# First expert's rows by products of 0/1 lists, experts of tiles 0 to 2 chosen ahead, weights not held back

## The reference

```python
def hier_moe(t, w_group, b_group, w_expert, b_expert, w_gate, w_up, w_down):
    g_logits = t @ w_group + b_group              # 4 groups
    g_w, g_idx = lax.top_k(softmax(g_logits), 1)
    e_logits = (t @ w_expert + b_expert).reshape(T, 4, 4)
    e_sel = take_along_axis(e_logits, g_idx)      # 4 experts of the group
    e_w, e_idx = lax.top_k(softmax(e_sel), 2)     # two of them
    weights = g_w * e_w / sum(e_w)
    for e in range(16):
        hdn = silu(t @ w_gate[e]) * (t @ w_up[e])     # 1024 -> 512
        y = y + combine[:, e:e+1] * (hdn @ w_down[e]) # 512 -> 1024
    return y
```

## Time and profile before

| | |
|---|---|
| median of 3 runs | 1140.63 us (1140.46 to 1142.6) |
| profiled execution | 1143.3 us, span 1141.5 us |
| PE busy | 1078.8 us (95% of the span), mean granted clock 0.98 |
| DVE, ACT, POOL busy | 508.6, 282.6, 265.0 us |
| DMA | 283.24 MB, mean 248 GB/s |
| expert stages | about 264 to 516 us (layer 0) and 850 to 1101 us (layer 1) |

### The profile page before, as it was taken

One profiled execution on the slowest core, in us unless ns is written; L12 is line 12 of the kernel. 1 busy time (PEld: TensorE's weight loads), 2 busy tenths in 40 slices (PEclk: granted clock), 3 DMA queues, 4 the chain that ended last, 5 costly groups with the idle time before them and its releaser, 6 DMA issues.

```text
span 1141.5 us, 17926 instructions
## 1 busy us (share of the span) xinstructions
PE 1078.8 (95%) x7469; PEld 647.0 (57%) x7469; DVE 508.6 (45%) x939; ACT 282.6 (25%) x461; POOL 265.0 (23%) x373
## 2 busy tenths in 40 slices
PE   6999999999999999996999999999989999999991
PEld 5688887874444433342788877777844444344430
DVE  3465237545533233326422357763355432343317
ACT  4442344320000000004232227763210000000012
POOL 1200012004333443123000013340023344433131
PEclk9899999999999999998999999999989999999996
DMA  9443311248999999998223210004279999999965
GB/s 322 127 146 112 106 38 74 110 186 331 402 422 421 422 423 423 423 418 288 102 75 111 79 69 1 2 1 166 71 263 415 419 421 421 422 423 423 423 230 198
DMA packets 68699, 283.24 MB, mean 248 GB/s; under 512 B 15048, under 2 KB 15216, under 8 KB 44064
## 3 DMA queue, kind: packets, MB, share of 16 engines
q1 hardware_dynamic: 47440, 239.32, 52.3%
q0 software_dynamic: 15232, 38.69, 9.4%
q10 hardware_dynamic: 5968, 4.40, 1.2%
HBM read 259.96 MB, written 22.41 MB: 247 GB/s over the span
## 4 chain that ended last, share of the span: by engine, by line
PE 81%; DVE 6%; DMA 4%; issue 4%; POOL 4%; ACT 1%; SPq 0%; POOLq 0%; DVEq 0%
PE ps L1843 41%; PE ps L1510 11%; PE ps L1512 10%; PE ps L1511 10%; DMA w_f<-in_m_w_up 2%; POOL xn_r L2295 1%; PE ps L1742 1%; DVE h L1384 1%; DMA xn<-output_table,pos 1%; PE ps L1520 1%; PE ps L1971 1%; DVE xn_r L1435 1%; POOL xn_r L2288 1%; PE ps L1654 1%; PE ps L1732 1%
## 5 line engine op out<-in xcount | busy, mean ns | idle before, releaser
L1843 PE MATMUL ps<-raw,s_f 128*32 128x256 f32 (+1 forms) x1536 | 175.8, 455 | 1.3 <-issue 0.7
L1843 PE MATMUL ps<-w_f,s_f 128*32 128x256 f32 (+1 forms) x1536 | 173.0, 451 | 2.6 <-issue 1.8
L1843 PE MATMUL ps<-xT_f,s_f 128*32 128x256 f32 (+1 forms) x1344 | 150.1, 451 | 0.4 <-DMA xT_f<-in_m_w_up 0.4
L1198 DVE TENSOR_TENSOR pad<-pad,ps 128x256 f32<-128x256 f32 x32 | 13.5, 421 | 296.6 <-ACT pad L790 296.6
L1843 PEld LDWEIGHTS ps<-raw,s_f 128*32 128x32 f32 (+1 forms) x1536 | 67.8, 119 | 103.5 <-issue 84.1
L1843 PEld LDWEIGHTS ps<-w_f,s_f 128*32 128x32 f32 (+1 forms) x1536 | 69.1, 119 | 95.4 <-issue 70.5
L1843 PEld LDWEIGHTS ps<-xT_f,s_f 128*32 128x32 f32 (+1 forms) x1344 | 59.7, 119 | 93.0 <-issue 74.0
L939 DVE SCALAR_TENSOR_TENSOR w_lo<-raw,gainT,w_hi 128x512 fp32r<-128x512 f32 x88 | 60.2, 746 | 105.3 <-ACT w_hi L594 105.3
L1208 DVE STREAM_TRANSPOSE s_f<-pad 32x128 f32<-32x128 f32 x256 | 103.0, 403 | 4.1
L1510 PE MATMUL ps<-w_hi,xT_hi 128*128 128x512 f32 x240 | 97.7, 407 | 5.9 <-DVE w_lo L939 2.9
L2252 POOL DMA_DIRECT2D output_table<-pad x60 | 33.7, 566 | 293.0 <-ACT pad L796 282.5
(11 more groups left out here) (299 smaller groups left out, 1470.8 us busy)
## 6 DMA issues: line engine op xcount, KB each, us to landing
raw<-in_m_w_down SPq DMA_DIRECT2D x28, 1024.0 KB
w_f<-in_m_w_down SPq DMA_DIRECT2D x28, 1024.0 KB
xT_f<-in_m_w_gate SPq DMA_DIRECT2D x26, 1024.0 KB
xT_f<-in_m_w_up SPq DMA_DIRECT2D x26, 1024.0 KB
raw<-in_m_w_gate SPq DMA_DIRECT2D x18, 1024.0 KB
raw<-in_m_w_up SPq DMA_DIRECT2D x18, 1024.0 KB
w_f<-in_m_w_gate SPq DMA_DIRECT2D x18, 1024.0 KB
w_f<-in_m_w_up SPq DMA_DIRECT2D x18, 1024.0 KB
```

Source lines behind the costliest of these rows:

```text
L1198: ve.tensor_tensor(hid2[:, 0:2 * P], sil2[:, 0:2 * P], ps[:, 0, 2 * P:4 * P], ALU.mult)
L1843: ins = te.matmul(ps[rows * n:rows * (n + 1), bank + kind, 0:width // parts], stationary(k, kind), weights(k, parts, n), start=k == 0, sto ...
```

## The change

1. Experts of tiles 0 to 2 are chosen (`select(0, 3)`, the comparisons of `router` before, a range of tiles at a time) between the halves of the last tile; `select(3, 4)` does the last tile after its logits. The ranks are likewise formed in two parts.
2. Expert 0's rows are no longer gathered. DVE writes a 0/1 matrix (`first_sel`, token by place) from each token's rank, and PE multiplies the normed rows `xn` on chip with it (`first_rows`: 4 tiles by 8 feature blocks, in float32), which gives the transposed rows at once. `up(0)` starts when the first half of them is copied.
3. The numbers of expert 1's tokens come by eight small products (`second_sel` with `id_parts`); its rows come by the token gather, and PE transposes them within `up(0)`, after its wide part. The lists of all experts and the numbers of the quarter rows are formed within `up(0)`, too. Expert 1's quarter gathers are gone.
4. The spare products `kept_warm` are gone.
5. SP no longer waits for the token gather ahead of p4. p6 now also waits until the products have read `xn`.

```diff
                 if p == OWN:
                     sp.wait_ge(A["rows_stored"], 16 * NT * (layer + 1))
+                    sp.wait_ge(E["x_tr"], 4 * layer + 2)
...
                     load_up(layer, p + 1, e, 1, g)
-                    if isinstance(e, int) and e == 1:
-                        sp.wait_ge(E["x_loaded0"], x_loads(layer, 0, -1))
                     load_down(layer, p + 2, e - 1, g)
...
+            def select(first, last):
+
+                tiles, quads4 = slice(first, last), slice(NR // NG * first, NR // NG * last)
+                n, by_tile = last - first, "p (i q) a -> p i q a"
+                fours = lg.rearrange("p i (q a) -> p (i q) a", a=NG)[:, quads4]
+                pairs = beats.rearrange("p (q n) -> p q n", n=NG * NG)[:, quads4]
+                table4 = beats.rearrange("p (q a b) -> p q a b", a=NG, b=NG)[:, quads4]
+                link(*[tt(pairs[:, :, d:d + (NG + 1) * (NG - 1 - d) + 1:NG + 1], fours[:, :, d:NG], fours[:, :, 0:NG - d], ALU.is_gt)
+                       for d in range(1, NG)])
+                link(red(row_sum[:, quads4], table4, AX.X, ALU.add),
+                     red(col_sum[:, quads4], table4.rearrange("p q a b -> p q b a"), AX.X, ALU.add))
+                link(tt(margin[:, quads4], row_sum[:, quads4], col_sum[:, quads4], ALU.subtract))
+                link(*[tt(is_k[:, k, quads4], margin[:, quads4], place[:, k, :].unsqueeze(1).broadcast_to([P, NR // NG * n, NG]), ALU.is_equal)
+                       for k in range(2)])
...
+                by_expert = "p (i e) -> p i e"
+                tt(sel_b[:, tiles, :], own[0].rearrange(by_expert, i=n), own[1].rearrange(by_expert, i=n),
+                   ALU.add).then_inc(V["sel_ready"], 1)
+
+            def places_of(sel, e, first, last):
+
+                return tt(sel[:, first:last, :], index_1[:, :].unsqueeze(1).broadcast_to([P, last - first, CAP]),
+                          rank_of_first[:, first:last, e:e + 1].broadcast_to([P, last - first, CAP]), ALU.is_equal)
+
+            def ranks_in(layer, first, last):
+
+                dve.wait_ge(M["ranks_done"], 2 * layer + (1 if first == 0 else 2))
+                link(stt(rank_of_first[:, first:last, :], ps[:, 6, 0:NT * NE].rearrange("p (i e) -> p i e", e=NE)[:, first:last, 0:2], 1.0,
+                         sel_b[:, first:last, 0:2], ALU.add, ALU.mult))
...
                 times_gain(0)
-                logits_in(j - 1)
+                link(logits_in(j - 1))
+                select(0, j)
                 add(j, 1)
+                ranks_in(layer, 0, j)
+                places_of(first_sel, 0, 0, j).then_inc(V["places_ready"], 1)
                 dve.wait_ge(M["hT_tr"], (NT + 1) * (layer + 1))
                 ve.tensor_copy(hT[j % 2][:, BN:D], ps[:, 1, :]).then_inc(V["hT_half"], 1)
...
             link(*[ve.memset(quarter[QUAD * n:QUAD * (n + 1), :], float(n)) for n in range(4)])
             tile_lo(0, 0)
+            dve.wait_ge(G["consts"], 2)
+            ve.tensor_copy(id_parts[:, :, :], token_id[:, :, 0:NT])
             dve.wait_ge(M["gains_tr"], 1)
...
-            def x_first(layer):
-                for f in (0, 1):
-                    dve.wait_ge(E["x_tr"], 2 * layer + (f + 1))
-                    ins = ve.tensor_copy(xe[0][:, 4 * f:4 * f + 4, :],
-                                         ps[:, 4 + f, 0:4 * CAP].rearrange("p (k c) -> p k c", k=4))
-                ins.then_inc(E["x_in"], 1)
+            def x_half(layer, n, f):
+                dve.wait_ge(E["x_tr"], 4 * layer + 2 * n + (f + 1))
+                return ve.tensor_copy(xe[n][:, 4 * f:4 * f + 4, :], ps[:, 4 + f, 0:4 * CAP].rearrange("p (k c) -> p k c", k=4))
...
                 B, I = blocks_of(layer), NE * layer
+                overflow_places(layer)
                 row_quarter_numbers(layer)
-                x_first(layer)
-                overflow_places(layer)
+                x_half(layer, 1, 0)
+                x_half(layer, 1, 1).then_inc(E["x_in"], 1)
...
+                last, by_expert = NT - 1, "p (i e) -> p i e"
+                select(last, NT)
+                places_of(second_sel, 1, 0, last)
+                ranks_in(layer, last, NT)
+                places_of(first_sel, 0, last, NT).then_inc(V["places_ready"], 1)
+                places_of(second_sel, 1, last, NT).then_inc(V["places_ready"], 1)
+                rank_e = ps[:, 6, 0:NT * NE]
                 by_choice = "p k (i e) -> p k (i e)"
                 link(tt(tmp_rank.rearrange("p (k i) e -> p k (i e)", k=2), oh,
                         rank_e.unsqueeze(1).broadcast_to([P, 2, NT * NE]), ALU.mult))
+                x_half(layer, 0, 0).then_inc(E["x_in"], 1)
                 link(red(rank_k, tmp_rank, AX.X, ALU.add))
+                ids(0, oh_k, NE)
+                ids(1, oh_k, NE)
                 tt(row_b[:, :, :], index[:, :].unsqueeze(1).broadcast_to([P, 2 * NT, CAP]),
...
                      *[tt(mm[:, NT * k:NT * (k + 1), :], oh[:, k, :].rearrange(by_expert, i=NT), lg[:, :, NG:NR], ALU.mult)
                        for k in range(2)],
-                     ve.tensor_copy(cnt, ps[:, 5, NT * NE:(NT + 1) * NE]))
+                     ve.tensor_copy(cnt, ps[:, 6, NT * NE:(NT + 1) * NE]))
...
                 tt(dd, m12[:, 1, :], m12[:, 0, :], ALU.subtract).then_inc(V["second_diff"], 1)
-                dve.wait_ge(M["lists_done"], 3 * layer + 1)
-                tokens_in(4, 0, NE)
+                dve.wait_ge(M["lists_done"], 4 * layer + 2)
+                tokens_in(7, 0, NE)
+                tt(list_f, ps[0:CAP, 7, 0:NE], token_f[:, 0:NE], ALU.add).then_inc(V["tokens_ready"], 1)
 
             def overflow_places(layer):
...
+                ranks(layer, range(last))
                 h_transposed_to(last, range(BK, KT))
+                pe.wait_ge(V["places_ready"], 5 * layer + 1)
+                pe.wait_ge(V["xn_ready"], NT * layer + last)
+                first_rows(EARLY[0:4])
                 logits(last, range(BK, KT))
...
+            EARLY = [(t, k) for f in (0, 1) for t in range(NT - 1) for k in range(4 * f, 4 * f + 4)]
+
+            def first_rows(products):
+
+                for t, k in products:
+                    at = CAP * (k % 4)
+                    ins = te.matmul(ps[:, 4 + k // 4, at:at + CAP], xn[:, t, every(KT, k)], first_sel[:, t, :],
+                                    start=t == 0 and k % 4 == 0, stop=t == NT - 1, skip_group_check=True)
+                return ins
+
+            def ranks(layer, tiles):
+
+                pe.wait_ge(V["sel_ready"], 2 * layer + (1 if tiles[0] == 0 else 2))
...
+                ins.then_inc(M["ranks_done"], 1)
+
             def x_transposed(S, i, loads):
...
 
-                def up(i, p, m, g=0, reuse=True):
-                    pe.wait_ge(E["x_in"], i + 1)
...
                                 pe.wait_ge(*pair_of(layer, p + n, g))
+                                if n and behind is not None:
+                                    pe.wait_ge(E["x_in"], x_ins(layer, i))
                             w = pair_slots[slot_of(p + n)]
...
+                                behind[n]()
 
                 def down(i, p, m, g=0):
...
-                up(I, 0, 0, 0, layer > 0)
-                lists(2 * layer + 2, 7, MAX_OVER)
+                def second_rows():
+
+                    pe.wait_ge(V["tokens_ready"], 4 * layer + 3)
+                    for group in range(GROUPS):
+                        for n in range(4):
+                            ins = te.matmul(ps[QUAD * n:QUAD * (n + 1), 6, NE * group:NE * (group + 1)],
+                                            ident[0:CAP, QUAD * group:QUAD * (group + 1)], list_f[:, :],
+                                            start=group == 0, stop=True, skip_group_check=True)
+                    ins.then_inc(M["lists_done"], 1)
+                    x_transposed(E, layer, x_loads(layer, 1, -1))
+
+                up(I, 0, 0, 0, layer > 0, (lambda: lists(5 * layer + 4, 7, NE), second_rows))
+                lists(5 * layer + 5, 7, MAX_OVER)
...
-            def kept_warm(n):
-
-                for _ in range(n):
-                    te.matmul(ps[:, 7, :], ident[:, :], h[:, 0, 0:BN], start=True, stop=True)
-
             def router(layer):
-                kept_warm(3)
-                pe.wait_ge(V["sel_ready"], layer + 1)
-                for i in range(NT):
...
-                ins.then_inc(M["ranks_done"], 1)
-                kept_warm(1)
-                lists(2 * layer + 1, 4, NE)
+                last = NT - 1
+                first_rows(EARLY[4:18])
+                ranks(layer, range(last, NT))
+                first_rows(EARLY[18:20])
+                pe.wait_ge(V["places_ready"], 5 * layer + 2)
+                pe.wait_ge(A["xn_scaled"], layer + 1)
+                first_rows((last, k) for k in range(4)).then_inc(E["x_tr"], 1)
+                first_rows(EARLY[20:])
+                first_rows((last, k) for k in range(4, KT)).then_inc(E["x_tr"], 1)
```

(49 more changed lines are left out.)

73 lines of the change are left out of this document (22 added, 51 removed).

## The result

The changed kernel takes 1159.2 us (median of 4 runs, 1158.28 to 1161.95), beside 1140.65 us of the kernel before on the same chip: ratio 1.0163, 95% interval 1.0142 to 1.0183. It is 18.5 us slower; 1138.5 us was forecast, with a range up to 1143.0. The profiled execution took 1159.6 us with a span of 1157.6.

What follows compares the result with a forecast made beforehand. PE was taken to bound the expert loop, weights close behind. Second-expert gains 1.3 + 2.1, less 2.0 for clock, plus 0.8 lag, less 0.1 start gave 2.1 us less: 1140.63 to 1138.5 us, range 1130.5 to 1143.

Steps and rivals of the forecast that it cites:

- The price of the products: Ahead of expert 0's up: 64 instructions at some 0.112 us cost 7.1 us; up(0) starts at 258.5, 5.95 us earlier.
- the rivals: Alternatives to the likeliest sum: transfers share evenly (0.13), between (0.15), transfers slower than taken (0.24), DMA is the bound (0.03).
- The gather decides: Within up(0): expert 1's rows land at 269.3 and 271.0 us, so PE waits 2.9 and 4.6 us.
- the slow rival: Released weights ahead of store and gather slow them to 9.5 and 10.0 us, giving 1144.5 us; chance 0.24.
- Loaded transfers: Behind 4 MB of queued weights, the last store takes 8.3 and 9.5 us, expert 1's gather 8.0 and 8.5.
- The choice of tiles 0 to 2: Before the last half of h: some 2.5 us fits DVE's 3.02 us gap; last tile's choice 1.7 instead of 2.95.
- The four first products: Beside the last tile's hT copy: hidden, or costing 0.2 us.
- Released weights: Expert 0's down weights and expert 2's first pair issue at about 247.7 us; less lag at late waits wins 0.8 us.
- The clock: After PE's wait for expert 1's gather: it may fall to 1.2 GHz, charged 1.0 us in each layer.

Runs made afterwards that it cites:

- a_contig: Changed kernel with each 0/1-list product reading 128 neighbouring columns instead of every eighth, expert 0's values then not the reference's; 1145.61 us, ratio 1.0050.
- c_rows: Changed kernel with expert 0's gate and up weights loaded in another row order, so products read neighbouring columns with right values; ratio 1.0044.
- b_released: Kernel before, without the wait that holds expert 0's down weights until the first gather has landed; 1160.5 us, ratio 1.0171.
- b_mid: Kernel before with the weight hold one pair later, ahead of expert 2's first pair, so only 2 MB are released; ratio 1.0069.
- b_choice: Kernel before with only the choice of tiles 0 to 2 and their ranks moved ahead of the last logits; ratio 1.0002.
- a_mid: Changed kernel, products still reading every eighth column, with weights from expert 2's first pair on held until expert 1's gather has landed; ratio 1.0111.
- a_tr_behind: Changed kernel with only expert 1's transposes put behind the narrow part of expert 0's up; ratio 1.0102.
- a_held: Changed kernel with the wait restored: expert 0's down weights and all behind them held until expert 1's gather has landed; ratio 1.0193.
- a_half: Changed kernel with 16 of the 32 products, those of tiles 1 and 2 left out, expert 0's x incomplete; ratio 1.0050.
- c_rows_held: Changed kernel with expert 0's weights reordered for neighbouring-column reads, and its down weights and all behind held until expert 1's gather landed; ratio 1.0012.

## Why the prediction was wrong

- **The price of the products** is the step that failed: "64 of them cost 7.1 us, and the 96 columns may make it less, never more at this clock". They cost 15.8. The row it went by had the same type and shape of stationary operand, but neighbouring columns; that the new one reads every eighth (`every(KT, k)`, in the diff) was not costed. With neighbouring columns the term is right: 28 in 3.19 us, the first `up` 0.1 us from the forecast. No end of the range was taken above 0.112, so the rivals all had PE early, and none had PE as the late one.
- **The gather decides**: right as a mechanism once the products are cheap (`a_contig`, `c_rows`: 4.4 to 5.0 us of waiting a layer), without part in the result, since PE came at 274.0. Its size was too small even so: landed at 271.6 instead of 269.3 (store 8.9 instead of 8.3, POOL 0.84 instead of 0.3, gather 9.1 from issue to landing instead of 8.0). After it transposes and narrow part took 6.8 us instead of 4.5, where 1.0 had been charged for the clock. This is the second step that failed, hidden by the first: even with cheap products the forecast would have been some 7 us too low (`a_contig` 1145.6 us, 1.0050; `c_rows` 1.0044) and out of its range. It is the mechanism of the slow rival, at the upper end of its times or just beyond.
- **Loaded transfers**: right for 4 MB in the queue (`b_released`). With 2 MB only the store is slow (`b_mid`).
- **The choice of tiles 0 to 2** fits the gap: hT copy 1.51 us after the last half of h, 1.44 before. It is worth nothing by itself (`b_choice`). The four first products, charged with 0.2, moved the last logits by 1.2 and 1.8 us with the dear read (from the hT copy to their read by VectorE 3.27 and 3.83 us instead of 2.05).
- **Released weights**: the 0.8 us can't be told apart; in all 0.5 us were won behind the second `up`'s groups. They are dear where a transfer on the path runs behind them.
- **The clock**: charged after a wait for the gather. It fell instead through the dear products with PE recorded busy all the time (+1.3 us in layer 0's first `up`), and again at the second `up`.

What is shown, in us of the 18.5: with the cheap read 13.5 of them go (`c_rows`, ratio 1.0163 to 1.0044), and with the hold one pair later 11 more (0.9945). With the dear read the second is worth 6, and by another way. **Open** is why silu of expert 0 is 1.8 us late in the changed kernel and the clock low in the second `up`: 8.1 us of its profiled execution (1.8 a layer of pause, 2.9 and 1.7 of the groups), and 6 and 7 us by the ratios of `a_mid` and `a_tr_behind`. Four edits (the hold one pair later, either operation behind, spare products) made it vanish, the full hold did not, both operations behind moved it on, and none names a cause. That PE is behind its records within the narrow part is shown by SP and ScalarE. That it ran the part at the lower clock would fit in length (the cold narrow part in `a_contig` took 5.23 us, and 3.59 + 1.7 is 5.3), but the granted clock of the profile speaks against it: 1.00 from 270 to 281 us. It is argued, not shown.

## What to carry to other kernels

A price is taken from a row with the same access pattern, not only the same shape and type: ask of each operand in which steps it is read. When an edit takes away a wait that keeps a queue empty, find the small transfers that ran in the gap: without the same line the kernel before lost 1.7%, since its gather was on the path, and the kernel whose PE was late anyway gained nothing by having it back. The best place lay, with the cheap read, between holding all and releasing all: one pair ahead, which slows the store but is through when the gather starts. In the kernel before, where a late store is a late gather, that place cost 0.7%.

## What was not expected of the hardware

- A weight load of 128 fp32 columns takes 192 ns by its row with neighbouring columns and 335 with every eighth; the pace per instruction goes from 0.114 to 0.243 us.
- The granted clock was 0.52 through 14 us in which PE was recorded busy for 14.00, in the dear products, and 0.50 with half of them; with all of the cheap ones it was 1.00.
- A store of 512 KB, 2.7 to 3.9 us with no weights released, took 6.7 to 8.2 us with 2 MB of weights issued some 5 us ahead of it and 7.6 to 8.9 us with 4 MB.
- By what SP and ScalarE saw of it, PE was 1.7 to 1.8 us behind its own records at the end of the narrow part of expert 0's `up`, in seven layers out of the eight of four kernels (the changed one, `a_held`, `a_half`, `c_rows_held`), and in no layer of the other kernels.
